# Attention with a maximum per chunk: a block's last exponential behind its stage's first tile, its factors behind the next block's first maximum

## The chip, the core and the metric

The kernel runs on one core of a Trainium2 chip. The metric is the time of one execution in microseconds (us) of device time. The core has five engines with a queue of their own each: TensorE (PE; PEld is its weight load), VectorE (DVE), ScalarE (ACT), GpSimd (POOL) and SyncE (SP), which issues nearly all DMAs. Each engine works through its queue in order; semaphores tie the queues together.

## What is computed

One decoder block over 2048 tokens of 1024 channels: a projection of the normalised input, a convolution branch, an attention branch with 8 heads, and a merge of both. The change touches the softmax of the attention branch alone:

```python
def block(args):                       # one block of 128 queries, all heads
    qn_b, qr_b, i = args
    scores = (einsum('bqhd,bkhd->bhqk', qn_b, k_nope)
              + einsum('bqhd,bkd->bhqk', qr_b, k_rope)) * scale
    scores = where(mask, scores, -inf)  # a query sees no later key
    p = softmax(scores, axis=-1)
    return einsum('bhqk,bkhd->bqhd', p, v)
```

## The kernel before

The attention stage (`attention_phase`, from L1142) works head by head: seven heads in a hardware loop, the eighth written out behind it (`last_body`). The 2048 queries are 16 blocks of 128, and four blocks form a group g; block b of group g sees g+1 chunks of up to 512 keys, and the last chunk is cut to (b+1)*128 keys. The groups come in the order 0, 3, 1, 2 (`ORDER`), so blocks s = 0 to 3 have one chunk, 4 to 7 four, 8 to 11 two, 12 to 15 three. A tile is a group's four blocks by 128 keys. The tiles of a head, T0 to T39, are 4 of g=0, 16 of g=3, 8 of g=1, 12 of g=2.

fp32 products are made of pairs in a rounded format: each operand is split in a high half (a copy on ScalarE) and a low half (a subtract on VectorE, or on GpSimd for the values and weights), and three products are added up. For one block the steps are:

- TensorE: `scores` (L1464), per chunk five products and, in the last chunk, the mask, into a bank of a ring of 5 (`ps_ring`). `ring_wait` lets a chunk start once the exponential five chunks before it is done (`exp_done`).
- VectorE, at the event `S`: the negative maximum per chunk (L1652, to `nmax`), then the least of these (L1658, to `nbias`, `max_done`). With one chunk, g=0, the first goes straight to `nbias`.
- ScalarE, at `E`: exp(score + nbias) from the bank to `prob`, with the row sum to `rsum` (L1586), for all chunks of the block. It waits for `max_done`.
- VectorE, at `E`: sum of the row sums (L1664) and reciprocal (L1670) to `rinv`.
- GpSimd, at `E`: each chunk of `prob` times `rinv` in place (L1719).

A tile at `T`: TensorE transposes it, 128x128 at a time (L1500), into one of two banks `ps_t`; ScalarE copies the high half (L1594, `pt_hi`), VectorE makes the low half (L1675, `pt_lo`). TensorE may transpose a tile once the `pt_lo` two tiles before it is done, and for the first tile that uses a chunk, once that chunk of the group's last block is normalised (`normed`). At `PV`, two tiles behind `T`, TensorE multiplies by the values (L1515 to L1517). At a group's last tile VectorE multiplies the sum by the gate (L1683), and SyncE stores it.

What sets the order is a list of events written out by `plan` (L1183) and `with_tail` (L1208). Every engine walks the same list and does its part of each event. Before, stage s of the list is S of block s, E of block s-1, and then a few tiles: 0, 1, 1, 2 in stages 4 to 7 (tiles T0 to T3), 0, 2, 7, 7 in stages 8 to 11 (T4 to T19), 0, 2, 3, 3 in stages 12 to 15 (T20 to T27). T28 to T39 come behind the list, between the next head's projections (QN, QR, K), in the last head straight behind it. The list also places `W` (splitting the next head's weights, stage 5), `VS` (splitting a quarter of the values, L1574 and L1710; stages 6 and 7 and the tail), and in the last head `OW` and `OA`: a piece of weights and the eight pieces of `o_v` that the output stage starts with (`o_a`: a copy on ScalarE, a subtract on VectorE). The `OA` pieces stand in pairs behind the events E of blocks 11 to 14. `o_v` is loaded once group 0 is stored.

## Time and profile before

| what | us |
|---|---|
| median of 3 runs (2697.78 to 2698.86) | 2698.16 |
| the profiled execution's own time | 2704.03 |
| its span, first to last instruction | 2702.2 |
| attention stage, TensorE's part of it | 1341 to 2165 |
| one head of the loop | 101.5 |
| TensorE busy | 2586.2 (96%) |
| VectorE busy | 1755.0 (65%) |
| ScalarE busy | 850.5 (31%) |
| GpSimd busy | 640.9 (24%) |

The rows below come from several views of the same execution. A row of the timeline gives the start in us from the span's start, the length in us, the engine, the line of the kernel, the operation with the buffers that it writes and reads, its shape, how many follow each other without a pause (x), and in brackets the idle time of the engine before it with what ended it. A row of the busy times gives a stretch, its length, the busy us of PE, PEld, DVE, ACT and POOL with the number of instructions, the granted TensorE clock as a share of full speed, and the share and GB/s of the DMA engines. Matmuls are pipelined: a 128x512 one shows a length of 0.39 us while the next starts 0.23 us behind it, so a short wait can hide in it.

### The profile page before, as it was taken

Reading aid. Unit: us, or ns where it says so; the run is one execution under the profiler, and the core shown is the slowest. Engines: PE = TensorE matmul, PEld = TensorE weight load, DVE = VectorE, ACT = ScalarE, POOL = GpSimd, SP = SyncE. Lnnn points to the kernel's source line nnn. Section 1 sums busy time; section 2 is a strip of 40 time slices with the busy share of each in tenths; the row PEclk is TensorE's granted clock in tenths of the full one; section 3 lists DMA queues with packets and bytes.
Section 4 is the critical chain, followed back from the end, with each engine's and each line's share of the span. In section 5 each row is a group of like instructions: output and inputs, shape, how many; then the busy total and the mean of one; then the engine's idle time right before and its main releaser. Section 6 shows DMA issues by size and latency. Waiting matters only on the chain. (4 is left out here: it accounts for less than half of the span.)

```text
span 2702.2 us, 32620 instructions
## 1 busy us (share of the span) xinstructions
PE 2586.2 (96%) x12186; PEld 2127.4 (79%) x12186; DVE 1755.0 (65%) x2073; ACT 850.5 (31%) x1683; POOL 640.9 (24%) x592
## 2 busy tenths in 40 slices
PE   4989999999999999997899999999999999999998
PEld 4767888888888888786677877877878778888887
DVE  5777967979779789564277667667677622223442
ACT  3432111111111111232255555555555520201221
POOL 3132111111111111232032232232232320323422
PEclk8999999999999999999899999999999999999999
DMA  8053212122112121376923112112112164666542
GB/s 298 8 164 116 78 47 78 47 67 83 53 55 78 47 78 48 124 243 240 278 73 107 62 60 107 62 60 107 61 61 86 55 202 156 205 215 211 190 149 78
DMA packets 200833, 306.74 MB, mean 114 GB/s; under 512 B 18234, under 2 KB 119678, under 8 KB 190621
## 3 DMA queue, kind: packets, MB, share of 16 engines
q1 hardware_dynamic: 194604, 284.89, 32.1%
q0 software_dynamic: 6128, 20.45, 2.4%
q8 instruction: 70, 1.15, 0.2%
q14 instruction: 31, 0.25, 0.0%
HBM read 202.01 MB, written 103.28 MB: 113 GB/s over the span
## 5 line engine op out<-in xcount | busy, mean ns | idle before, releaser
L52 PE MATMUL ps_proj<-h_hi,w_hi 128*128 128x512 f32 x1696 | 670.6, 395 | 9.0 <-DVE h_lo L697 6.8
L54 PE MATMUL ps_proj<-h_hi,w_lo 128*128 128x512 f32 x1696 | 663.1, 391 | 0.0
L53 PE MATMUL ps_proj<-h_lo,w_hi 128*128 128x512 f32 x1696 | 663.0, 391 | 0.0
L812 DVE SCALAR_TENSOR_TENSOR acc<-u,taps_t,acc 128x2048 f32<-128x2048 f32 x240 | 629.0, 2621 | 8.5
L52 PEld LDWEIGHTS ps_proj<-h_hi,w_hi 128*128 128x128 f32 x1696 | 320.7, 189 | 77.9 <-issue 8.0
L53 PEld LDWEIGHTS ps_proj<-h_lo,w_hi 128*128 128x128 f32 x1696 | 320.7, 189 | 67.9 <-issue 2.5
L54 PEld LDWEIGHTS ps_proj<-h_hi,w_lo 128*128 128x128 f32 x1696 | 320.2, 189 | 67.4
L586 POOL TENSOR_TENSOR w_lo<-raw,w_hi 128x1024 fp32r<-128x1024 f32 x53 | 168.4, 3177 | 808.5 <-ACT w_hi L411 808.4
L1719 POOL TENSOR_SCALAR prob<-prob,rinv 128x512 f32<-128x512 f32 (+2 forms) x320 | 199.0, 638 | 352.3 <-DVE rinv L1670 352.1
L1675 DVE TENSOR_TENSOR pt_lo<-ps_t,pt_hi 128x512 fp32r<-128x512 f32 (+1 forms) x320 | 194.1, 609 | 96.8 <-ACT pt_hi L1594 93.1
L1594 ACT ACTIVATE pt_hi<-ps_t 128x512 fp32r<-128x512 f32 (+1 forms) x320 | 169.4, 532 | 237.6 <-PE ps_t L1500 237.6
L1652 DVE TENSOR_REDUCE nmax<-ps_ring 128x1 f32<-128x512 f32 (+3 forms) x288 | 174.6, 622 | 96.1 <-PE ps_ring L1485 78.0
L539 ACT ACTIVATE lat<-ps_proj 128x512 f32<-128x512 f32 x128 | 76.3, 598 | 493.6 <-PE ps_proj L54 429.2
L2005 DVE TENSOR_TENSOR o_y<-o_ps,o_g 128x512 f32<-128x512 f32 x64 | 43.9, 690 | 265.2 <-PE o_ps L54 201.2
L1586 ACT ACTIVATE prob<-ps_ring,nbias 128x512 f32<-128x512 f32 (+2 forms) x320 | 195.3, 625 | 37.5 <-DVE nbias L1658 33.1
L52 PE MATMUL o_ps<-o_a_hi,o_w_hi 128*128 128x512 f32 x512 | 199.8, 390 | 3.4 <-DVEq L1996 3.4
L53 PE MATMUL o_ps<-o_a_lo,o_w_hi 128*128 128x512 f32 x512 | 199.9, 390 | 0.0
L54 PE MATMUL o_ps<-o_a_hi,o_w_lo 128*128 128x512 f32 x512 | 199.8, 390 | 0.0
L1500 PE MATMUL ps_t<-ident,prob 128*128 128x128 f32 x1088 | 173.3, 275 | 14.9 <-POOL prob L1719 9.5
L1500 PEld LDWEIGHTS ps_t<-ident,prob 128*128 128x128 f32 x1088 | 131.4, 141 | 48.2 <-POOL prob L1719 12.2
L1515 PE MATMUL ps_o<-pt_hi,v_hi 128*128 128x512 f32 (+1 forms) x320 | 141.4, 442 | 0.7 <-DVE bg L1683 0.7
L1480 PE MATMUL ps_ring<-kn_hi,qn_hi 128*128 128x512 f32 (+2 forms) x320 | 125.3, 392 | 8.4 <-ACT prob L1586 5.0
(220 smaller groups left out, 4037.8 us busy)
## 6 DMA issues: line engine op xcount, KB each, us to landing
qlat<-qlat_dram SPq DMA_DIRECT2D x32, 1024.0 KB, 5.9
raw<-in_w_in_dram SPq DMA_DIRECT2D x52, 512.0 KB, 6.4
under_h<-in_w_ada_dram SPq DMA_DIRECT2D x8, 1024.0 KB, 11.2
ga_dram<-lat SPq DMA_DIRECT2D x8, 1024.0 KB, 5.0
gb_dram<-lat SPq DMA_DIRECT2D x8, 1024.0 KB, 5.0
agate_dram<-lat SPq DMA_DIRECT2D x8, 1024.0 KB, 5.0
conv_dram<-acc SPq DMA_DIRECT2D x8, 1024.0 KB, 3.9
bgate_dram<-lat SPq DMA_DIRECT2D x8, 1024.0 KB, 5.0
```

The lines of the kernel that those rows point to most:

```text
L52: pe.matmul(out, wh, xh, start=first, stop=False)
L53: pe.matmul(out, wh, xl, start=False, stop=False)
L54: return pe.matmul(out, wl, xh, start=False, stop=last)
L586: pool.tensor_tensor(weights(tile)[1][:], raw[tile % 2][:], weights(tile)[0][:].bitcast(F32), ALU.subtract).then_inc(lo_made, 1)
L812: dve.scalar_tensor_tensor(acc[:], u[:, n:n + S], tap(n), acc[:], ALU.mult, ALU.add).then_inc(conv_tap if n < TAPS - 1 else conv_done, 1)
L1500: mm = pe.transpose(ps_t[:, n % 2, b * P:(b + 1) * P], prob[:, x:x + P], k.ident[:])
L1515: pe.matmul(out, v_hi[:, j, :], mh, start=(j == 0), stop=False)
L1586: act.activation(prob[:, x:x + width], ps[:, chunk_no[n, c] % RING, 0:width], ACT.Exp, bias=nbias[:, n:n + 1], accum_out=rsum[:, n, c:c + ...
L1594: act.activation(pt_hi[n % SLOTS][:, s], ps_t[:, n % 2, s], ACT.Copy).then_inc(t_hi, 1)
L1652: ins = dve.tensor_reduce(to, ps[:, chunk_no[n, c] % RING, 0:width], AX.X, ALU.max, negate=True)
L1675: dve.tensor_tensor(pt_lo[n % SLOTS][:, s], ps_t[:, n % 2, s], pt_hi[n % SLOTS][:, s].bitcast(F32), ALU.subtract).then_inc(t_lo, 1)
L1719: pool.tensor_scalar(prob[:, x:x + width], prob[:, x:x + width], rinv[:, n:n + 1], 1.0, ALU.mult, ALU.mult).then_inc(normed, 1)
```

## The change

The exponential of a chunk of g > 0 no longer uses the maximum of the block but the chunk's own (bias `nmax[:, n, c]`), and waits for that alone (`max_step`). The chunk's share, exp(chunk maximum - block maximum), is made by a small extra exponential on ScalarE over the g+1 chunk maxima (`share_of`). VectorE's `factors` multiplies the chunk sums by the shares, adds them, takes the reciprocal, and multiplies the shares by it: four dependent small steps where there were two. GpSimd then scales each chunk by its own factor. For g = 0 there is one chunk, and only the reciprocal remains.

In the list, E of block s moves from stage s+1 to stage s, in two parts: `EA`, all chunks but the last, straight behind `S`, and `E`, the last chunk and the shares, behind the stage's first tile if it has one (on ScalarE behind that tile's high half). VectorE's factors of block s-1, which stood behind all maxima of block s, now stand behind its first one. `R` is the last block's factors and scaling, behind the last stage's tiles. `W`, `VS`, `OW` and `OA` stand behind E as before, so the last head's `OA` pieces move one stage earlier with it: pairs in stages 11 (behind T13), 12, 13 (behind T20) and 14 (behind T22).

```diff
--- before.py
+++ after.py
@@ -1193,16 +1193,18 @@
 
         share = {3: [0, 1, 1, 2], 1: [0, 2, 7, 7], 2: [0, 2, 3, 3]}
         for s, (g, b) in enumerate(BLOCKS):
-            ev.append(("S", s))
-            if s:
-                ev.append(("E", s - 1))
+            ev += [("S", s), ("EA", s)]
+            n = share[g][b] if g in share else 0
+            if n:
+                tiles(1)
+                n -= 1
+            ev.append(("E", s))
             if s == 5:
                 ev.append(("W", 0))
             if s in (6, 7):
                 ev.append(("VS", s - 4))
-            if g in share:
-                tiles(share[g][b])
-        ev.append(("E", len(BLOCKS) - 1))
+            tiles(n)
+        ev.append(("R", len(BLOCKS) - 1))
         return ev, tiles, pend
 
     def with_tail(last):
@@ -1265,6 +1267,7 @@
         nmax = sb("nmax", [P, 16, NC_], F32)
         nbias = sb("nbias", [P, 16], F32)
         rsum = sb("rsum", [P, 16, NC_], F32)
+        share_of = sb("share_of", [P, 16, NC_], F32)
         rinv = sb("rinv", [P, 16], F32)
         ps = ctx.enter_context(nc.psum_tensor("ps_ring", [P, RING, TC], F32))
         ps_t = ctx.enter_context(nc.psum_tensor("ps_t", [P, 2, TC], F32))
@@ -1289,6 +1292,7 @@
         max_done = sem("max_done")
         exp_done = sem("exp_done")
         sum_step = sem("sum_step")
+        share_done = sem("share_done")
         rinv_done = sem("rinv_done")
         normed = sem("normed")
         t_done = sem("t_done")
@@ -1573,19 +1577,26 @@
                                                              + PV_CREDIT))
                             act.activation(v_hi[:, n * QB:(n + 1) * QB, :], v_raw[n % 2][:],
                                            ACT.Copy).then_inc(v_hi_made, 1)
-                        elif kind == "E":
+                        elif kind in ("EA", "E"):
                             g, b = BLOCKS[n]
-                            act.wait_ge(max_done, at.block(n + 1))
-
-                            if b == 0:
+                            n_max = chunk_no[n, 0] - QB
+                            if b == 0 and kind == "EA":
                                 held = {0: 0, 3: 0, 1: first_tile[3], 2: first_tile[1]}[g]
                                 act.wait_ge(t_done, at.tile(held + T_CREDIT))
-                            for c in range(g + 1):
+                            for c in range(g) if kind == "EA" else (g,):
                                 width = TC if c < g else (b + 1) * P
                                 x = (p_at(g, b) + c * QB) * P
+                                if g:
+                                    act.wait_ge(max_step, at.i * (N_CHUNK - QB) + n_max + c + 1)
+                                else:
+                                    act.wait_ge(max_done, at.block(n + 1))
                                 act.activation(prob[:, x:x + width], ps[:, chunk_no[n, c] % RING, 0:width], ACT.Exp,
-                                               bias=nbias[:, n:n + 1],
+                                               bias=nmax[:, n, c:c + 1] if g else nbias[:, n:n + 1],
                                                accum_out=rsum[:, n, c:c + 1]).then_inc(exp_done, 1)
+                            if g and kind == "E":
+                                act.wait_ge(max_done, at.block(n + 1))
+                                act.activation(share_of[:, n, 0:g + 1], nmax[:, n, 0:g + 1], ACT.Exp, scale=-1.0,
+                                               bias=nbias[:, n:n + 1]).then_inc(share_done, 1)
                         elif kind == "T":
                             g, j = TILES[n]
                             s = slice(max(0, j - QB * g) * P, TC)
@@ -1602,6 +1613,23 @@
             def _(dve):
                 dve.sem_inc(t_lo, LO_CREDIT)
                 dve.sem_inc(o_done, O_CREDIT)
+
+                def factors(at, n):
+                    g, b = BLOCKS[n]
+                    dve.wait_ge(exp_done, at.scores(chunk_no[n, g] + 1))
+                    if g:
+                        done = at.i * (3 * (16 - QB)) + 3 * (n - QB)
+                        sums, shares = rsum[:, n, 0:g + 1], share_of[:, n, 0:g + 1]
+                        dve.wait_ge(share_done, at.i * (16 - QB) + (n + 1 - QB))
+                        dve.tensor_tensor(sums, sums, shares, ALU.mult).then_inc(sum_step, 1)
+                        dve.wait_ge(sum_step, done + 1)
+                        dve.tensor_reduce(rinv[:, n:n + 1], sums, AX.X, ALU.add).then_inc(sum_step, 1)
+                        dve.wait_ge(sum_step, done + 2)
+                        dve.reciprocal(rinv[:, n:n + 1], rinv[:, n:n + 1]).then_inc(sum_step, 1)
+                        dve.wait_ge(sum_step, done + 3)
+                        dve.tensor_scalar(shares, shares, rinv[:, n:n + 1], None, ALU.mult).then_inc(rinv_done, 1)
+                    else:
+                        dve.reciprocal(share_of[:, n, 0:1], rsum[:, n, 0:1]).then_inc(rinv_done, 1)
 
                 def run(ev, at, prol=False):
                     number = order_of(ev)
@@ -1652,22 +1680,15 @@
                                 ins = dve.tensor_reduce(to, ps[:, chunk_no[n, c] % RING, 0:width], AX.X, ALU.max,
                                                         negate=True)
                                 ins.then_inc(max_step if g else max_done, 1)
+                                if n and c == 0:
+                                    factors(at, n - 1)
                             if g:
                                 n_max = chunk_no[n, g] + 1 - QB
                                 dve.wait_ge(max_step, at.i * (N_CHUNK - QB) + n_max)
                                 dve.tensor_reduce(nbias[:, n:n + 1], nmax[:, n, 0:g + 1], AX.X,
                                                   ALU.min).then_inc(max_done, 1)
-                        elif kind == "E":
-                            g, b = BLOCKS[n]
-                            dve.wait_ge(exp_done, at.scores(chunk_no[n, g] + 1))
-                            if g:
-                                dve.tensor_reduce(rinv[:, n:n + 1], rsum[:, n, 0:g + 1], AX.X,
-                                                  ALU.add).then_inc(sum_step, 1)
-                                dve.wait_ge(sum_step, at.i * (16 - QB) + (n + 1 - QB))
-                                src = rinv[:, n:n + 1]
-                            else:
-                                src = rsum[:, n, 0:1]
-                            dve.reciprocal(rinv[:, n:n + 1], src).then_inc(rinv_done, 1)
+                        elif kind == "R":
+                            factors(at, n)
                         elif kind == "T":
                             g, j = TILES[n]
                             s = slice(max(0, j - QB * g) * P, TC)
@@ -1709,14 +1730,15 @@
                             v = slice(n * QB, (n + 1) * QB)
                             pool.tensor_tensor(v_lo[:, v, :], v_raw[n % 2][:], v_hi[:, v, :].bitcast(F32),
                                                ALU.subtract).then_inc(v_lo_made, 1)
-                        elif kind == "E":
+                        elif kind == "R" or kind == "S" and n:
+                            n -= kind == "S"
                             g, b = BLOCKS[n]
                             pool.wait_ge(rinv_done, at.block(n + 1))
                             pool.sem_inc(passed, 1)
                             for c in range(g + 1):
                                 width = TC if c < g else (b + 1) * P
                                 x = (p_at(g, b) + c * QB) * P
-                                pool.tensor_scalar(prob[:, x:x + width], prob[:, x:x + width], rinv[:, n:n + 1], 1.0,
+                                pool.tensor_scalar(prob[:, x:x + width], prob[:, x:x + width], share_of[:, n, c:c + 1], 1.0,
                                                    ALU.mult, ALU.mult).then_inc(normed, 1)
 
                 run(prologue, At(-1), prol=True)
```

## Rows read from the trace of the kernel before

**Rows 1.** Busy time of the second head: start:end, its length, then each engine.

```profile
1462.48:1564.04 101.56, 99.24 (x546) 81.63 (x546) 72.67 (x149) 56.48 (x139) 31.36 (x45) 1.00 0.22 76
```

**Rows 2.** Waits of TensorE, attention stage: total us, times, longest us.

```profile
PE ps_t L1500 <- POOL prob L1719: 9.5, 9, 3.2
PE ps_ring L1480 <- ACT prob L1586: 5.0, 24, 0.3
```

**Rows 3.** Timeline of TensorE, block 5: start us, length us, engine, line, operation.

```profile
1472.04 0.40 PE L1485 MATMUL ps_ring<-kr_lo,qr 128*128 128x512 f32 x1
1472.70 0.50 PE L1480 MATMUL ps_ring<-kn_hi,qn_hi 128*128 128x512 f32 x1 [0.26 <-ACT prob L1586]
1473.03 0.39 PE L1481 MATMUL ps_ring<-kn_lo,qn_hi 128*128 128x512 f32 x1
1473.26 0.40 PE L1482 MATMUL ps_ring<-kn_hi,qn_lo 128*128 128x512 f32 x1
```

**Rows 4.** Timeline of TensorE: T4, the first tile of g=3.

```profile
1492.62 0.66 PE L1500 MATMUL ps_t<-ident,prob 128*128 128x128 f32 x4 [0.78 <-POOL prob L1719]
```

**Rows 5.** Timeline of GpSimd: blocks 7 and 8 are normalised.

```profile
1491.87 3.71 POOL L1719 TENSOR_SCALAR prob<-prob,rinv 128x512 f32<-128x512 f32 x6
```

**Rows 6.** Timeline of VectorE, block 10.

```profile
1495.34 0.68 DVE L1683 TENSOR_TENSOR bg<-ps_o,bg 128x512 f32<-128x512 f32 x1
1495.94 1.16 DVE L1652 TENSOR_REDUCE nmax<-ps_ring 128x1 f32<-128x512 f32 x2
...
1497.21 0.14 DVE L1664 TENSOR_REDUCE rinv<-rsum 128x1 f32<-128x2 f32 x1
1497.39 0.16 DVE L1670 RECIPROCAL rinv<-rinv 128x1 f32<-128x1 f32 x1
1497.62 0.69 DVE L1675 TENSOR_TENSOR pt_lo<-ps_t,pt_hi 128x512 fp32r<-128x512 f32 x1
```

**Rows 7.** Timeline of ScalarE in the output stage: a small activation and its follower.

```profile
2566.76 0.29 ACT L1960 ACTIVATE o_ss<-o_ss,eps 128x1 f32<-128x1 f32 x1
2566.96 1.66 ACT L1935 ACTIVATE o_a_hi<-o_v 128x512 fp32r<-128x512 f32 x3
```

**Rows 8.** Timeline of ScalarE, last head, blocks 13 and 14.

```profile
2130.07 0.60 ACT L1594 ACTIVATE pt_hi<-ps_t 128x512 fp32r<-128x512 f32 x1 [0.20 <-PE ps_t L1500]
2130.57 0.68 ACT L1586 ACTIVATE prob<-ps_ring,nbias 128x512 f32<-128x512 f32 x1
...
2131.23 0.69 ACT L1586 ACTIVATE prob<-ps_ring,nbias 128x512 f32<-128x512 f32 x1
...
2131.89 0.48 ACT L1586 ACTIVATE prob<-ps_ring,nbias 128x256 f32<-128x256 f32 x1
...
2132.34 1.17 ACT L1562 ACTIVATE o_a_hi<-o_v 128x512 fp32r<-128x512 f32 x2
```

**Rows 9.** Timeline of TensorE: end of two chunks, and T8 and T24.

```profile
1490.77 0.39 PE L1485 MATMUL ps_ring<-kr_lo,qr 128*128 128x512 f32 x1
...
1498.62 0.49 PE L1500 MATMUL ps_t<-ident,prob 128*128 128x128 f32 x3
...
1518.79 0.39 PE L1485 MATMUL ps_ring<-kr_lo,qr 128*128 128x512 f32 x1
...
1526.77 0.60 PE L1500 MATMUL ps_t<-ident,prob 128*128 128x128 f32 x4
```

**Rows 10.** Timelines of GpSimd and VectorE at one time.

```profile
1464.02 1.29 POOL L1710 TENSOR_TENSOR v_lo<-v_raw,v_hi 128x512 fp32r<-128x512 f32 x1 [7.82 <-ACT v_hi L1574]
...
1464.11 1.74 DVE L1640 TENSOR_TENSOR qr<-rope_a,qr 64x512 fp32r<-64x512 f32 x1
```

**Rows 11.** Timeline of TensorE, last head: T27.

```profile
2144.41 0.33 PE L1500 MATMUL ps_t<-ident,prob 128*128 128x128 f32 x1 [0.95 <-DVE pt_lo L1675]
```

**Rows 12.** TensorE in the last head: T28, and the stretch behind it.

```profile
2148.45 0.66 PE L1500 MATMUL ps_t<-ident,prob 128*128 128x128 f32 x4 [3.19 <-POOL prob L1719]
...
2149.20:2156.00 6.80, 6.14 (x24) 5.05 (x23) 2.92 (x5) 2.39 (x4) 0.53 (x1) 0.50 0.16 54
```

## The prediction

> **What bounds the kernel now.** I read the busy time by head first. The second head takes 101.56 us and TensorE is busy for 99.24 of it at full clock; VectorE is busy for 72.67 and ScalarE for 56.48 [rows 1]. So the attention stage is bound by TensorE's matmuls, and the change alters no matmul. All it can do is remove or add waits of TensorE. Next I read what TensorE waits for in this stage, over all eight heads. It waits for a normalised piece of `prob` 9 times, 9.5 us in all, one of them 3.2 us, and for an exponential that frees a bank of the score ring 24 times, 5.0 us [rows 2]. Then I read TensorE in order of time around each wait, since part of a wait hides in the modelled length of a matmul; the distance between starts is the better measure. Below, blocks are s = 0 to 15 and tiles T0 to T39 of a head in the order of the lists; all times are of the second head unless said.
>
> *Ring waits.* Neighbouring 512-column matmuls start 0.23 us apart (1473.03 to 1473.26). Before the second chunk of block 5 the distance is 0.66 us, and 0.33 behind it, so this wait costs 0.43 + 0.10 = 0.53 us [rows 3]. The like places in blocks 6 and 7 cost 0.47 and 0.44 by the same distances. Block 4's (0.39) hangs on the head's first exponential. That is not moved, so it stays.
>
> *The wait for GpSimd.* T4, the first tile of g=3, starts at 1492.62 after 0.78 us of shown idle [rows 4]; by the distance of starts it is 0.95, and 0.05 in the next transposes: 1.00 us. GpSimd ran from 1491.87 on block 7's chunks [rows 5], and in before's order a v_lo piece stood in front of them on its queue.
>
> **What the change takes away, per head.** Chunks 0 to 2 of a four-chunk block now go through the exponential as soon as their own maximum is known, within the block's own stage. The bank that the next block's second chunk wants is free more than 1 us early. Gone: 0.53 + 0.47 + 0.44 = 1.44 us. Block 7's factors are computed behind the first maximum of block 8. That maximum ends at about 1490.1, v_lo holds GpSimd to about 1490.3, the four small steps end at 1490.9, and the first chunk is normalised at 1491.6. T4 wants it at 1491.68 (0.94 before 1492.62): the wait falls to 0.05. Gone: 0.95. Sum of the gains: **2.4 us per head**.
>
> **What it adds, per head: small steps on two queues.**
> VectorE: per block of g>0 a multiply over 2 to 4 columns and a multiply by a pointer scalar, beside the sum and reciprocal that were there. No row shows such small multiplies; the nearest are the sum and the reciprocal. Dependent steps follow at 0.18 us (1497.21 to 1497.39), the work behind the last at about 0.08 [rows 6]. Old: 0.26. New: 3 x 0.19 + 0.08 = 0.65. The extra is 0.39 us; bounds 0.2 (a step at half) and 1.2 (each new step held up by GpSimd once, below). All four now stand between the first and second maximum.
> ScalarE: per block an exponential of 2 to 4 values. Nearest row: a 128x1 activation with a bias takes 0.29 and the next begins 0.20 behind its start [rows 7]. I take 0.20; bounds 0.08 (a 512-column copy's 0.49 less 512 columns' worth) and 0.29.
> 12 blocks have these, 4.7 and 2.4 us per head of engines with 29 and 45 us idle. As sums they cost nothing. As links of a chain they may cost: a tile's copy (ScalarE) and remainder (VectorE) stand on the same queues, and the tile two places on cannot be transposed before.
>
> *The wait at T8.* Other lengths: 512 exponential to next 0.67, 256 columns 0.45, copy 0.60 (to next 0.49) [rows 8]; maximum or remainder 0.69 (to next 0.61), gate multiply to next 0.60 [rows 6]. A finished engine releases the next in 0.04, and TensorE in 0.15. Block 9's first chunk leaves TensorE at 1491.16 [rows 9]. Maximum to 1491.90. Factors of block 8: 1491.82 to 1492.47, or to 1492.93 with GpSimd's hold-up. Maximum of 256 columns to 1493.41. Last exponential from 1493.45, share from 1493.90, copy of T5 1494.10 to 1494.70, remainder 1494.73 to 1495.42, gate multiply from 1495.34, block 10's first maximum 1495.94 to 1496.63. Its exponential from 1496.67, copy of T6 1497.33 to 1497.93, remainder 1497.96 to 1498.65. T8 can start at 1498.80. Without T4's wait TensorE would want T8 at 1498.62 - 0.94 = 1497.68. So it waits **1.12**, and 0.11 follows: 1.23 us. Without GpSimd's hold-up 0.75. In the old order this copy stood ahead of the block's exponentials, so the cover was there.
>
> *The hold-up.* VectorE's 64x512 subtract with two inputs in SBUF usually takes 0.69, but 1.74 where GpSimd's 1.29 us operation had started 0.09 before it, and it ended 0.54 behind that one [rows 10]. Factor steps that fall into GpSimd's run of block 7's four chunks should wait likewise: 0.46 in the walk. The Trainium skill ("SBUF — State Buffer", Who interferes with whom) says that a VectorE instruction with two SBUF inputs, or a tensor_scalar in its two-port mode, and a GpSimd instruction that reads SBUF exclude each other for the whole instruction. By that rule both new multiplies would be held and T8 waits 1.12; the trace agrees for two inputs and shows nothing for the pointer multiply.
>
> *The wait at T24.* Block 13's second chunk leaves TensorE at 1519.18. The factors of block 12 hold VectorE to 1519.33. Maximum to 1520.02; exponential from 1520.06; copy of T20 1520.73 to 1521.33; last exponential (256) 1521.22; share 1521.67; copy of T21 1521.87 to 1522.47; remainder to 1523.19; gate multiply from 1523.11; block 14's first maximum 1523.71 to 1524.40; factors to 1524.97; second maximum to 1525.66; exponential from 1525.70; copy of T22 1526.37 to 1526.97; remainder to 1527.69; T24 at 1527.84. Now it starts at 1526.77 [rows 9], so it waits **1.07**, with 0.06 behind. T16 comes out 0.08 late; T27 is in time.
>
> **Sum.** Per head -2.39 + 1.23 + 1.13 + 0.08 = +0.05: the waits change place. Seven heads: +0.3.
> *Last head.* It has two waits of its own, at T24 and T27 (0.95 shown at T27 [rows 11], 1.05 and 1.17 by starts). They come from the o_a pieces, two copies in 1.17 us on ScalarE [rows 8] and as many subtracts on VectorE behind each pair, and they move. Gone with the rest: 2.4 + 1.05 + 1.17. T28's wait (3.19 shown, 3.36 by starts [rows 12]) falls to about 1.8, as block 15's exponentials are done before its last tiles. Sum 6.2. Added: the 1.23 at T8; T16 1.3, since two o_a pieces now stand in front of T14's copy; T23 1.0; T24 3.5, as four pieces delay blocks 13 and 14 by 2 us each way. Sum 7.0 to 7.4. Net +1.0. Behind the 3.19 us of idle the granted clock was 0.50 for 6.8 us [rows 12]; I expect one such stretch again, behind T24 in place of T28: no difference. If it falls out, 3.2 us are gained; if there are two, 3 lost.
> Against the profiled run (2704.03): 2704.03 + 0.3 + 1.0 = 2705.3. That run is 5.9 above the median of 2698.16, so I forecast **2699.5**.
>
> **The rivals.**
> *B, the new waits are small.* Both walks end on ScalarE and VectorE steps 0.04 to 0.2 long that I can't see. If shares cost 0.08, the factor steps 0.1 each, and GpSimd holds nothing, T8's and T24's waits come to half: 8 x 1.2 = 9.6, so 2698.2 - 9.6 = 2689 (2685 to 2692). For it: VectorE is idle for 29 us a head, and much of that lies in front of the second maxima, where TensorE needs 1.14 us a chunk and VectorE 0.61. Against: the walks have no idle step.
> *C, slower: factors in front of the second maximum.* Where GpSimd is still normalising, each of the two multiplies may wait a whole chunk (0.62), and the second maximum, its exponential and the next tile's copy move with it. Its place is blocks 8 to 10, and 13 to 14 through the gate multiply. It decides once the factors of block 8 take more than 1.1 us, or those of 13 more than 0.65. At 0.6 us more in each head at either place: 8 x 1.2 = 9.6, so 2708 (2704 to 2712).
> *D, the ring waits stay,* because an exponential now waits for its own chunk's maximum, while the new waits come: 8 x 1.4 = 11, so 2710. Against: by the walk the bank is free over 1 us early.
>
> **Chances.** Forecast (2693 to 2704) 0.47, B 0.28, C 0.20, D 0.05. Range 8 in 10: 2687 to 2709. A measurement here can tell 0.2% (5.4 us) from no change: faster below 2692.8, slower above 2703.6. Faster 0.28, same 0.47, slower 0.25.
>
> **What would show it.** Right: no wait for an exponential at the second chunks of blocks 5 to 7, T4's wait below 0.2, and in every head new waits for pt_lo of 0.8 to 1.3 us at T8 and T24; heads of 101.3 to 102.0 us. B: such waits below 0.6 and heads near 100.3. C: above 1.5 and heads over 102.5. The four factor steps should lie 0.19 apart where GpSimd is idle, and be stretched in block 8's. The forecast fails if a wait that I did not walk opens elsewhere (T16, T27, the first projections of the next head), or if the o_v load has not landed when ScalarE reaches the first o_a piece, one stage earlier than now.

## The result: 2706.65 us, slower by 0.27%

The changed kernel takes 2706.65 us (median of 8 runs, 2705.14 to 2708.09) where the kernel before takes 2699.05 in the same comparison. The ratio is 1.0027, with an interval of 1.0017 to 1.0037: 4.6 to 10 us slower. The forecast was 2699.5, so the time is inside the range and on the slower side of the forecast, where I had put a chance of 0.25.

The profiled execution took 2707.97 us, against 2704.03 before. That difference (3.9) is smaller than the one in the medians (7.6). The stage that the change touches gives a cleaner one: from the first score to the end of the last head's last product it takes 804.3 us before (1360.96 to 2165.29) and 810.5 after (1358.81 to 2169.29), so **6.2 us more**. Ahead of attention, where nothing was changed, the changed kernel's profiled run is 2.2 us shorter, and that is why the profiled executions differ by less.

The page of the changed kernel, its span and the busy time of its engines:

```profile
span 2706.2 us, 33319 instructions
PE 2577.3 (95%) x12186; PEld 2122.9 (78%) x12186; DVE 1800.8 (67%) x2265; ACT 873.8 (32%) x1779; POOL 639.9 (24%) x592
```

The second and the last head of the changed kernel, by windows (stretch, its length, busy time and instructions of PE, PEld, DVE, ACT and POOL, granted clock, DMA share, GB/s):

```profile
1461.55:1563.88 102.33, 98.58 (x547) 81.68 (x546) 78.42 (x173) 59.45 (x151) 31.51 (x45) 1.00 0.22 76
2075.65:2169.29 93.64, 83.78 (x474) 68.24 (x473) 67.23 (x159) 56.05 (x146) 30.74 (x44) 1.00 0.19 63
```

The second head has grown from 101.56 [rows 1] to 102.33 us; a head is counted from its first score to that of the next. TensorE has no more work, but VectorE has 78.42 where it had 72.67. The other heads follow: the first one 102.74 (101.52 before), the five behind the second 102.33 to 102.37. The last one is 93.64 (93.50 before). By heads: 1.2 + 6 x 0.8 + 0.14 = 6.1 of the 6.2 us.

What the tiles and their products wait for in the attention stage, all heads (total us, times, longest):

```profile
PE ps_t L1504 <- POOL prob L1741: 17.0, 17, 1.9
PE ps_t L1504 <- DVE pt_lo L1696: 13.8, 17, 1.9
PE ps_o L1519 <- DVE bg L1704: 3.1, 3, 2.2
```

Before, the exponentials' ring waits stood here with 24 entries and `prob` with 9.5 us [rows 2]. The ring waits are gone. The wait for GpSimd's `prob`, which was to vanish, has grown to 17.0, in 17 places instead of 9.

### The profile page after: what moved, and what is told of

Its sections match the earlier page's. It is cut to its first block and busy times, and to the rows that moved or that the text cites. A ratio compares the mean times of both kernels' runs of the same rounds, so it can differ in the third digit from the quotient of the medians.

```text
span 2706.2 us, 33319 instructions
## 1 busy us (share of the span) xinstructions
PE 2577.3 (95%) x12186; PEld 2122.9 (78%) x12186; DVE 1800.8 (67%) x2265; ACT 873.8 (32%) x1779; POOL 639.9 (24%) x592
## 5 line engine op out<-in xcount | busy, mean ns | idle before, releaser
L1741 POOL TENSOR_SCALAR prob<-prob,share_of 128x512 f32<-128x512 f32 (+2 forms) x320 | 196.2, 628 | 323.5 <-DVE share_of L1630 305.2
L1593 ACT ACTIVATE prob<-ps_ring,nmax 128x512 f32<-128x512 f32 (+3 forms) x288 | 182.2, 634 | 151.8 <-DVE nmax L1680 150.9
```

The source lines that it names most:

```text
L1593: act.activation(prob[:, x:x + width], ps[:, chunk_no[n, c] % RING, 0:width], ACT.Exp, bias=nmax[:, n, c:c + 1] if g else nbias[:, n:n + 1 ...
L1741: pool.tensor_scalar(prob[:, x:x + width], prob[:, x:x + width], share_of[:, n, c:c + 1], 1.0, ALU.mult, ALU.mult).then_inc(normed, 1)
```

## The second head, wait by wait

TensorE in order of time (start, length, then the idle time before it and its releaser in brackets): the second chunk of block 5, then T4, T8 and T24.

```profile
1470.71 0.39 PE L1489 MATMUL ps_ring<-kr_lo,qr 128*128 128x512 f32 x1
1470.94 0.40 PE L1484 MATMUL ps_ring<-kn_hi,qn_hi 128*128 128x512 f32 x1
...
1490.58 0.66 PE L1504 MATMUL ps_t<-ident,prob 128*128 128x128 f32 x4 [1.59 <-POOL prob L1741]
...
1497.15 0.52 PE L1504 MATMUL ps_t<-ident,prob 128*128 128x128 f32 x3 [0.42 <-POOL prob L1741]
...
1526.59 0.63 PE L1504 MATMUL ps_t<-ident,prob 128*128 128x128 f32 x4 [0.96 <-DVE pt_lo L1696]
```

The starts at block 5's second chunk are 0.23 apart where they were 0.66 [rows 3]. T4 shows 1.59 where it showed 0.78 [rows 4], and T8 and T24 [rows 9] now wait. By distance of starts, in us:

| place | before | forecast | after |
|---|---|---|---|
| ring waits, blocks 4 to 7 | 1.85 | 0.39 | 0 |
| T4 | 1.00 | 0.05 | 1.81 |
| T8 | 0 | 1.23 | 0.58 |
| T16 | 0 | 0.08 | 0.05 |
| T24 | 0 | 1.13 | 1.13 |

The differences add up: -1.85 + 0.81 + 0.58 + 0.05 + 1.13 = +0.72 of the head's +0.77.

*T8's releaser* is named GpSimd, but VectorE's remainder of T6 ends at 1497.00, 0.15 before T8's start:

```profile
1496.31 0.69 DVE L1696 TENSOR_TENSOR pt_lo<-ps_t,pt_hi 128x512 fp32r<-128x512 f32 x1
```

That is the gap at which TensorE follows VectorE here; GpSimd's `prob` had long been there. This is the chain that the forecast walked.

*T4's releaser* is GpSimd in earnest. GpSimd in order of time, with its idle time before each step:

```profile
1476.87 1.84 POOL L1723 TENSOR_TENSOR head_w_l<-head_raw,head_w_h 128x768 fp32r<-128x768 f32 x1 [1.74 <-ACT head_w_h L1550]
1478.95 2.48 POOL L1741 TENSOR_SCALAR prob<-prob,share_of 128x512 f32<-128x512 f32 x4 [0.24 <-DVE share_of L1630]
1482.54 1.29 POOL L1731 TENSOR_TENSOR v_lo<-v_raw,v_hi 128x512 fp32r<-128x512 f32 x1 [1.12 <-ACT v_hi L1578]
...
1487.66 1.29 POOL L1731 TENSOR_TENSOR v_lo<-v_raw,v_hi 128x512 fp32r<-128x512 f32 x1 [1.01 <-ACT v_hi L1578]
1489.83 3.71 POOL L1741 TENSOR_SCALAR prob<-prob,share_of 128x512 f32<-128x512 f32 x6 [0.88 <-DVE share_of L1630]
```

VectorE's factor steps over the same time:

```profile
1472.32 0.23 DVE L1630 TENSOR_SCALAR share_of<-share_of,rinv 128x4 f32<-128x4 f32 x1
...
1477.23 1.51 DVE L1630 TENSOR_SCALAR share_of<-share_of,rinv 128x4 f32<-128x4 f32 x1
1478.65 1.74 DVE L1680 TENSOR_REDUCE nmax<-ps_ring 128x1 f32<-128x512 f32 x3
...
1482.87 0.99 DVE L1630 TENSOR_SCALAR share_of<-share_of,rinv 128x4 f32<-128x4 f32 x1
...
1487.99 0.68 DVE L1680 TENSOR_REDUCE nmax<-ps_ring 128x1 f32<-128x512 f32 x1
1488.59 0.38 DVE L1624 TENSOR_TENSOR rsum<-rsum,share_of 128x4 f32<-128x4 f32 x1
```

The pointer multiply over 4 columns takes 0.23 when GpSimd is free. Block 4's does. Block 5's takes 1.51: GpSimd's `head_w_l` subtract began 0.36 before it and ended at 1478.71, and the multiply ended at 1478.74. Block 6's takes 0.99 and ends 0.03 behind the v_lo subtract (1483.83, 1483.86). Behind each stand the second, third and fourth maximum of the next block, and behind these its exponentials. ScalarE shows it:

```profile
1463.02 1.28 ACT L1593 ACT_TABLE_LOAD   x1
1465.27 0.37 ACT L1593 ACTIVATE prob<-ps_ring,nbias 128x128 f32<-128x128 f32 x1 [0.96 <-DVE nbias L1680]
...
1479.37 0.69 ACT L1593 ACTIVATE prob<-ps_ring,nmax 128x512 f32<-128x512 f32 x1 [1.82 <-DVE nmax L1680]
```

It sits 1.82 us for a maximum. All that follows is late: the copies for `VS`, thus GpSimd's v_lo at 1487.66, the remainder at 1487.78, block 8's first maximum at 1487.99. The late v_lo then lies over the first factor step (0.38 instead of 0.15). The factors are done at 1489.6, GpSimd starts at 1489.83, and T4 at 1490.58.

The first two rows bear on block 4's ring wait, which I had left standing. The table load of the exponentials now begins at 1463.02 and is over when the first maximum comes. In the kernel before it ran behind the wait for that maximum:

```profile
1466.28 1.28 ACT L1586 ACT_TABLE_LOAD   x1 [2.33 <-DVE nbias L1652]
1467.57 0.37 ACT L1586 ACTIVATE prob<-ps_ring,nbias 128x128 f32<-128x128 f32 x1
```

The likely reason is that the diff swaps two waits in front of this exponential. `max_done` came first, then `t_done`; now `t_done` stands in `EA` and `max_done` in `E`. The load would stand behind the first wait and ahead of the second in both. No run tried this alone, so the reason is not shown. With the load out of the way block 4's 0.39 us is gained, which no step of the forecast holds.

## The experiments

Two accounts stood against each other. **P:** the last factor step, a multiply by a pointer scalar, is held by GpSimd's long subtracts, and this is T4's wait. **Its rivals:** the new order on ScalarE, in which a block's exponentials stand between a tile's two copies, or the mere length of the small steps. Each expectation says what either account would give. Head lengths below are those of the second head (before 101.56, after 102.33), and waits of tiles are by distance of starts. The diffs show the main lines of each edit, with other lines left out. Run 4 edits the kernel before and run 8 the kernel of run 5, the others edit the changed kernel. Runs 1 to 9 were executed once each.

The changed kernel holds one such comparison itself. Its last head has no next head's weights to split, so `head_w_l` is not there. Block 5's multiply is not held in it, only block 6's (0.98 us), and T4 waits 0.51 instead of 1.81.

**1. No pointer multiply on VectorE.** GpSimd's instruction takes both factors, so the step falls out.

```diff
-                        dve.tensor_scalar(shares, shares, rinv[:, n:n + 1], None, ALU.mult).then_inc(rinv_done, 1)
-                                pool.tensor_scalar(prob[:, x:x + width], prob[:, x:x + width], share_of[:, n, c:c + 1], 1.0,
+                                pool.tensor_scalar(prob[:, x:x + width], prob[:, x:x + width], rinv[:, n:n + 1],
+                                                   share_of[:, n, c:c + 1] if g else 1.0,
```

> The changed kernel without VectorE's last factor step: GpSimd's scaling takes the reciprocal and the chunk's share as its two scalars. In the changed kernel that step took 1.51 us in block 5 and 0.99 in block 6 (0.23 elsewhere), ending 0.03 behind a GpSimd operation. Theory P (VectorE's last step is shut out by GpSimd's long subtracts, the second maxima and all behind them slip, and with them block 7's normalising): those 1.3 and 0.8 us vanish, T4's wait falls from 1.76 us to at most 0.4, T8's rises from 0.58 towards 1.1 as TensorE is no longer late, T24's stays at 1.0 to 1.13; heads of 101.2 to 101.6 us instead of 102.36. Rival Q (the places in the queues do it: v_lo stands behind the later exponentials, and the port has no part): T4's wait stays above 1.3 us and heads at 102.2 or more.

It took 2694.46 us in one run, beside 2702.51 for the kernel before. Its second head:

```profile
1459.51:1560.02 100.51, 98.54 (x547) 81.71 (x546) 75.31 (x161) 60.13 (x151) 34.45 (x45) 1.00 0.22 77
```

T4's wait is down from 1.81 to 0.12, T24's fell from 1.13 to 0.74, and T8's is 0.78. The rival by which the places in the queues do it, with T4 above 1.3, is out: those places are the same here. The step that is removed is worth 1.8 us a head. GpSimd pays with 34.45 busy us instead of 31.51. The gain is larger than expected: the four-step chain became three, so T24 profits as well.

**2. Factors behind the last maximum,** not the first.

```diff
-                                if n and c == 0:
-                                    factors(at, n - 1)
+                            if n:
+                                factors(at, n - 1)
```

> The changed kernel with VectorE's factors of the block before behind all maxima of a block, as in the kernel before; all else as changed. Theory P: a held step no longer stops the maxima, so T4's wait falls from 1.76 to 0.3 to 0.7 us (block 7's factors come 0.3 later than they could). Of the chain that ends at T24 the 0.65 us of factors before the second maximum of block 14 and 0.11 in block 13 fall out: T24's wait 1.13 goes to about 0.4. T8's about 0.5. Heads near 100.9 us. Rival Q: T4's wait stays above 1.3 us; T24's falls all the same.

It took 2705.2 us, and its second head 102.03 instead of the expected 100.9. One row of its VectorE, then two of its GpSimd:

```profile
1484.87 1.39 DVE L1630 TENSOR_SCALAR share_of<-share_of,rinv 128x4 f32<-128x4 f32 x1
```
```profile
1484.41 0.59 POOL L1741 TENSOR_SCALAR prob<-prob,share_of 128x384 f32<-128x384 f32 x1
1484.96 1.28 POOL L1731 TENSOR_TENSOR v_lo<-v_raw,v_hi 128x512 fp32r<-128x512 f32 x1
```

T24's wait fell to 0.32, as expected: the steps no longer stand in front of the second maximum. In its place T15 waits 0.28 and T27 0.47. T4's did not fall to the expected 0.3 to 0.7; it is 1.75, which is the rival's condition. Block 7's own multiply is held here, and ends 0.02 behind v_lo. But that is not what makes T4 late: v_lo stands in front of block 7's chunks on GpSimd's own queue until 1486.24, and GpSimd starts on them at 1486.47, so the held multiply costs T4 about 0.2. The late factors of block 6 had pushed v_lo there: GpSimd sat 1.25 us idle for them, and v_lo followed their chunks without a pause. So the place that helps T24 makes GpSimd's queue late. What this run says of T4 is neither for P nor against it.

**3. No shares at all** (and two factor steps as before). This kernel leaves out the weighting of the chunks: each is scaled by the reciprocal of the plain sum, which is not the softmax. It gives the price of the small steps.

```diff
-                                act.activation(share_of[:, n, 0:g + 1], nmax[:, n, 0:g + 1], ACT.Exp, scale=-1.0,
-                                               bias=nbias[:, n:n + 1]).then_inc(share_done, 1)
-                        dve.tensor_tensor(sums, sums, shares, ALU.mult).then_inc(sum_step, 1)
-                        dve.tensor_scalar(shares, shares, rinv[:, n:n + 1], None, ALU.mult).then_inc(rinv_done, 1)
```

> Leaves out the shares: each chunk is scaled by the reciprocal of the plain sum, so the chunks of a row are weighted wrongly; 12 small exponentials per head on ScalarE and 24 small multiplies on VectorE are gone, the order is that of the changed kernel. It gives the price of the small steps. Theory (both steps as links of the chain to T24: 0.20 of share, 0.39 and 0.11 of factors): T24's wait falls from 1.13 to about 0.4; T4's to at most 0.3, as nothing of VectorE is shut out. Heads near 100.7 us. Rival: the order alone makes the waits (a tile's copy behind the exponentials of its own block): T24 stays above 0.9.

It took 2684.09 us, with a second head of 99.69: the small steps together cost 2.6 us a head. T4 waits 0 and T24 0.36, where 0.4 was expected. T8 still waits 0.60, where run 5, with T4's wait all but gone too, has 0.80. So two thirds of T24's wait are made by the small steps, and three quarters of T8's are not: they are left to the new order of exponentials and copies.

**4. The kernel before, with its v_lo splits earlier,** in stages 4 and 6 instead of 6 and 7. It has none of the new small steps, so it shows how much of the wait at T4 before came from GpSimd's queue.

```diff
-            if s in (6, 7):
-                ev.append(("VS", s - 4))
+            if s in (4, 6):
+                ev.append(("VS", 2 + (s == 6)))
```

> The kernel before with the values' splits moved from stages 6 and 7 to 4 and 6, so that no v_lo stands in front of block 7's scaling on GpSimd. If T4's wait of 0.95 us there comes from that alone, it goes to 0.0 to 0.1 us, heads of 100.6 us instead of 101.55, 7 to 8 us in all; if it comes from block 7's late exponentials, it stays above 0.7.

It took 2697.26 us. Its second head took 101.06 where 100.6 was expected. Its GpSimd, then its TensorE, at T4:

```profile
1488.26 2.04 POOL L1719 TENSOR_SCALAR prob<-prob,rinv 128x512 f32<-128x512 f32 x3 [0.62 <-DVE rinv L1670]
```
```profile
1489.01 0.55 PE L1500 MATMUL ps_t<-ident,prob 128*128 128x128 f32 x3 [0.20 <-POOL prob L1719]
```

GpSimd no longer has v_lo in front of the chunks: it sits 0.62 us idle for the reciprocal, and VectorE had in turn waited for the block's last exponential. T4's wait fell from 1.00 to 0.42 and not to nothing. So of the wait of before, GpSimd's queue made about 0.6, and the block's late exponentials the rest.

**5. The changed kernel with its splits early.** The same change that P asks for: `W` and `VS` directly behind `S`, ahead of the exponentials, so that GpSimd's subtracts are over when the factors come.

```diff
             ev.append(("S", s))
+            if s == 5:
+                ev.append(("W", 0))
+            if s in (6, 7):
+                ev.append(("VS", s - 4))
```

> The changed kernel with W and the two VS events directly behind S instead of behind E, so that ScalarE copies the weights and values ahead of the block's exponentials and GpSimd's long subtracts end before VectorE's factor steps. All factor steps stay. Theory P (a factor step that meets a GpSimd operation waits for its end): the last step takes 0.23 us in blocks 4 to 7, no second maximum slips, T4's wait falls from 1.76 to 0.0 to 0.3 us, T8's rises to 0.8 to 1.1, T24's stays 1.1; heads of 100.8 to 101.4 us. Rival Q (the added step and its place alone, with no shut-out): heads as in the changed kernel, 102.3.

It took 2697.33 us (before 2698.06). The pointer multiply over all heads (count, then shortest, median and longest in ns), first in the changed kernel, then with the splits early:

```profile
L1630 DVE TENSOR_SCALAR share_of<-share_of,rinv x96: 228/229/1516, 1369.9 to 2153.4; 128x4 f32<-128x4 f32 x32, 128x2 f32<-128x2 f32 x32, 128x3 f32<-128x3 f32 x32
```
```profile
L1631 DVE TENSOR_SCALAR share_of<-share_of,rinv x96: 228/229/277, 1368.4 to 2143.4; 128x4 f32<-128x4 f32 x32, 128x2 f32<-128x2 f32 x32, 128x3 f32<-128x3 f32 x32
```

The longest falls from 1516 to 277 ns, T4's wait from 1.81 to 0.16, and the head from 102.33 to 101.16. T24 stays at 1.13. T8 rises to 0.80, since TensorE now comes to it earlier, and 0.20 appears at a product behind T4. P holds: all small steps are there and in their places, and with the overlap gone nearly all of T4's wait is gone. This edit changes ScalarE's order too and alone would leave the rival standing; run 1 keeps that order.

**6. Odd columns.** The multiply over 4 columns is cut in 3 and 1, to see whether the hold-up depends on an even width.

```diff
-                        dve.tensor_scalar(shares, shares, rinv[:, n:n + 1], None, ALU.mult).then_inc(rinv_done, 1)
+                        for part in (slice(0, 3), slice(3, 4)) if g == 3 else (slice(0, g + 1),):
+                            ins = dve.tensor_scalar(share_of[:, n, part], share_of[:, n, part], rinv[:, n:n + 1], None,
+                                                    ALU.mult)
```

> The changed kernel with the last factor step of a four-chunk block in two parts, three columns and one. It asks which form of that step GpSimd can shut out. If only an even number of elements can use VectorE's second port (a two-port mode), the parts are not held: 0.16 to 0.23 us each in blocks 5 and 6, T4's wait falls to 0.4 or less, heads near 101.4 us. If any pointer multiply is held, the first part takes the 1.5 and 1.0 us as before and heads stay at 102.3 to 102.5.

It took 2711.88 us with a head of 102.74, slower than the changed kernel. The same view as above:

```profile
L1631 DVE TENSOR_SCALAR share_of<-share_of,rinv x128: 199/228/1510, 1367.4 to 2156.5; 128x3 f32<-128x3 f32 x64, 128x1 f32<-128x1 f32 x32, 128x2 f32<-128x2 f32 x32
```

The longest is still 1510 ns, and it is a part of three columns (8 of them at 0.97 to 0.99, 7 at 1.50 to 1.51). An odd width does not escape, and the added instruction makes T4's wait longer, 2.18.

**7. The o_a pieces later.** In the last head they go behind the next stage's `S`, as late as before.

```diff
-                ev.insert(ev.index(("E", 11 + t // 2)) + 1 + t % 2, ("OA", t))
+                ev.insert(ev.index(("S", 12 + t // 2)) + 1 + t % 2, ("OA", t))
```

> The changed kernel with the last head's o_a pieces one stage later (behind S of blocks 12 to 15), where they stood before the change in time. Theory: the waits of the last head at T16 (1.34), at the first product of T20 (2.41) and at T24 (2.09) come from these pieces. T16's goes to below 0.1; the other two together from 4.5 to 2.5 or less, with about 1 us new at T27: the last head is 2.5 to 4 us shorter than 93.6 us; the others are unchanged at 102.3.

It took 2704.3 us. Its last head:

```profile
2074.00:2165.60 91.60, 83.54 (x474) 68.20 (x473) 68.03 (x159) 56.36 (x146) 33.15 (x44) 1.00 0.20 64
```

The last head is 2.0 us shorter than after's 93.64, less than the 2.5 to 4 expected. The wait at T16 is down to 0.11 and the one of the product is gone, but T24 now waits 2.78 and T27 1.10. The pieces have to be copied and subtracted somewhere; they moved the wait more than they removed it.

**8. One tile ahead of the exponentials,** on top of 5. If T8's wait came from the exponentials standing ahead of the first tile's copy, this would end it.

```diff
+            if n:
+                tiles(1)
+                n -= 1
             ev.append(("EA", s))
-            if n:
-                tiles(1)
-                n -= 1
             ev.append(("E", s))
```

> The kernel of run splits_early with a stage's first tile ahead of the block's exponentials (S, tile, EA, E, other tiles). It tests the order on ScalarE's queue, with all small steps kept. Theory (T8 and T24 wait because the copy of T6 and T22 stands behind exponentials of its own block): T24's wait falls from 1.13 to below 0.2 and T8's from 0.80 to below 0.2; the second tile's copy now stands behind all of them, so T9 and T15 or T16 wait 0.4 to 0.8 each; small ring waits (0 to 0.3) can return at blocks 6 and 7. Heads of 100.2 to 101.0 us instead of 101.16. Rival (the small steps make the waits, wherever the copy stands): T24 stays above 0.7.

This expectation failed. It took 2728.33 us, with a second head of 104.30. T24 waits 1.25 and T8 0.72, neither below the expected 0.2; T16 waits 0.72, T4 1.33, and ring waits are back at blocks 6 and 7. The largest waits of that head, then one row of its ScalarE and one of its VectorE:

```profile
PE ps_t L1505 <- DVE pt_lo L1697: 2.1, 3, 1.1
PE ps_t L1505 <- POOL prob L1742: 1.7, 2, 1.1
PE ps_ring L1485 <- ACT prob L1594: 0.4, 2, 0.2
```
```profile
1493.32 0.29 ACT L1606 ACTIVATE pt_hi<-ps_t 128x128 fp32r<-128x128 f32 x1
```
```profile
1493.64 0.29 DVE L1697 TENSOR_TENSOR pt_lo<-ps_t,pt_hi 128x128 fp32r<-128x128 f32 x1 [2.32 <-ACT pt_hi L1606]
```

The first tile's copy is early, but the second one's now stands behind all of the block's exponentials and the share. VectorE waits 2.32 us for it, and with VectorE all the maxima behind. So moving the exponentials to the other side of the first copy does not end the wait. The recorded rival, by which the small steps make the waits wherever the copy stands, has its condition met (T24 above 0.7), but by run 3 T8 keeps 0.60 without those steps. That the waits come from exponentials standing between two copies of one stage at all fits the rows; no run tests it alone.

**9. The mixture.** Blocks 0 to 7 as changed (early exponentials, chunk maxima), with both factors on GpSimd and the splits early. Few tiles compete for ScalarE there. Blocks 8 to 15 in the order of before, with one maximum and one factor.

```diff
+            if s < EARLY:
+                ev.append(("EA", s))
+                ...
+                ev.append(("E", s))
+            elif s > EARLY:
+                ev += [("EA", s - 1), ("E", s - 1)]
```

> A mixture: blocks 0 to 7 as in the changed kernel (maximum by chunk, own stage), but with GpSimd applying both factors and the splits directly behind S; blocks 8 to 15 in the order of the kernel before (block maximum, exponentials one stage later, sum and reciprocal behind the maxima). Theory: the ring waits (1.85 us) and T4's wait (0.95) are gone and no wait at T8 and T24 comes, since there the tile's copy stands ahead of its own block's exponentials again: heads of 98.6 to 99.2 us, the whole about 20 us below the kernel before. Rival: T8's and T24's waits come from the state in which blocks 5 to 7 leave the queues, and stay at 0.5 or more: heads above 99.8.

It took 2678.29 us in one run. Its second head, and what TensorE waits for in it:

```profile
1455.81:1554.50 98.69, 97.94 (x546) 81.87 (x546) 74.11 (x153) 57.91 (x143) 32.89 (x45) 1.00 0.22 78
```
```profile
PE ps_t L1509 <- DVE pt_lo L1701: 0.5, 1, 0.5
PE ps_ring L1489 <- DVE kn_lo L1653: 0.3, 1, 0.3
```

The ring waits, T4's, T8's and T24's are all gone. What is left is T32's, which before has too. The head is 2.87 us shorter than before's, and the waits of before that are gone are 1.85 + 1.00 = 2.85. Its edit changes the order, the small steps and the splits together, so it does not say which of them frees T8 and T24. But it shows that the gains that I forecast were there to be had; the held multiply and the new waits at T8 and T24 gave them back.

**10 to 12. Timed.** The mixture again, the kernel of run 1, and the mixture with the last head's o_a pieces each behind one of the last eleven tiles (`OA` t behind tile T(29+t)).

> The mixture of run early_group3 again, timed: its heads were 98.68 us against 101.55, so 8 x 2.87 = 23 us at most and 19.8 in that single look. Theory: 0.9915 to 0.9935 of the kernel before.

> The changed kernel with the chunk's two factors applied by GpSimd, timed: heads of 100.5 us against 101.55. Theory: the change's only loss was the last factor step shut out by GpSimd, so without that step it is faster than the kernel before, 0.996 to 0.998. Rival: the last head takes back what the seven give, 0.999 or more.

> The mixture with the last head's o_a pieces behind tiles T29 to T36 instead of in stages 12 to 15. Theory: the waits at T24 (1.06) and T27 (1.12) of the last head vanish, VectorE's two 0.6 us steps per tile against TensorE's 1.13 cost 0.1 a tile in the tail, so 1 to 2 us less than the mixture. Rival: the tail becomes bound by VectorE and the output stage starts no earlier: no difference.

| kernel | median us | ratio to before (2699.42) |
|---|---|---|
| both factors on GpSimd | 2691.75 | 0.9969, 0.9957 to 0.9981 |
| mixture | 2678.41 | 0.9927, 0.9914 to 0.9941 |
| mixture, o_a at the tail | 2675.65 | 0.9911, 0.9898 to 0.9925 |

All three are faster than both kernels of this case. The last two can't be told apart by their intervals, but their last heads can. First the mixture's, then that with the pieces at the tail:

```profile
2045.90:2138.10 92.20, 86.19 (x474) 71.48 (x473) 62.37 (x140) 55.12 (x138) 34.81 (x44) 0.94 0.20 64
```
```profile
2048.85:2138.50 89.65, 84.91 (x474) 70.22 (x473) 62.52 (x139) 54.92 (x138) 31.93 (x44) 0.96 0.21 65
```

The difference of 2.55 us is about that of the medians (2.8), where 1 to 2 were expected. The waits at T24 and T27 are gone, which are the forecast's 1.05 and 1.17; besides, a product behind them waits 0.6 longer, and the stretch at half clock is shorter. Such a stretch is left in each: the granted clock is 0.50 from 2120 to 2125 in the first, and 0.61 in the mean from 2120 to 2128 in the second. The attention stage of the last kernel takes 780.9 us against 804.3, 23.4 less; the medians differ by 23.8.

## Where the forecast held and where it failed, by its own steps

The time lies in the range, but the reason given for it failed at T4, and that the whole still fits is partly luck, as the last head shows.

**Right: the ring waits.** They went, by more than counted: 1.85 a head, not 1.44. The step "Block 4's (0.39) hangs on the head's first exponential. That is not moved, so it stays" failed. The exponential wasn't moved, but the load of its table was.

**Wrong: T4.** "T4 wants it at 1491.68: the wait falls to 0.05" is the step that failed, and the one that decided. It came to 1.81 in each of the seven heads of the loop, an error of 1.76 us, and to 0.51 in the last. The walk took GpSimd's v_lo as something in front of the chunks on GpSimd's queue, and did not look at what GpSimd's subtracts do to VectorE. The text had the mechanism and its upper bound ("each new step held up by GpSimd once"), but placed it at block 8 alone, where GpSimd scales. The factors of blocks 5 and 6 and the subtracts `head_w_l` and v_lo, which the change had moved behind `E` with everything else, I never laid side by side. The shown price is 0.76 to 1.28 us for a step of 0.23, where I had 0.46. Run 1 takes away the step and run 5 the overlap, and T4's wait is down to 0.12 and 0.16. In run 2 the step is held at another place, where v_lo on GpSimd's own queue was the larger hindrance.

The Trainium skill ("SBUF — State Buffer", Who interferes with whom) says that a VectorE tensor_scalar in its two-port mode and a GpSimd instruction exclude each other for the whole instruction. The trace agrees: 0.99 and 1.51 instead of 0.23, ended 0.03 behind GpSimd. The forecast drew on this rule and applied it to one place of three. By the same page the one that issues first has the ports. In run 2 the multiply's row begins 0.09 before v_lo's and is yet held for 1.39; but GpSimd's chunk of 1484.41 was still running until 1484.99, and v_lo followed it without a pause. So that row is no case of VectorE coming first. The Trainium skill ("VectorE: DVE Perf Modes", What auto-detection actually checks) lets odd widths into this mode if source and destination are equal. Run 6 agrees, with three columns at 1.51.

**Half right: T8.** Forecast 1.23, or 0.75 without GpSimd's hold-up; measured 0.58 behind T4's wait, and 0.80 where that is gone (run 5). The hold-up of 0.46 in block 8's factors did not come in the seven heads of the loop, though GpSimd was scaling just then. It came in the last head. The multiply with two inputs and the GpSimd chunk beside it, first in the second head, then in the last:

```profile
1490.49 0.70 POOL L1741 TENSOR_SCALAR prob<-prob,share_of 128x512 f32<-128x512 f32 x1
1490.56 0.15 DVE L1624 TENSOR_TENSOR rsum<-rsum,share_of 128x2 f32<-128x2 f32 x1
...
2103.29 0.70 POOL L1741 TENSOR_SCALAR prob<-prob,share_of 128x512 f32<-128x512 f32 x1
2103.39 0.60 DVE L1624 TENSOR_TENSOR rsum<-rsum,share_of 128x2 f32<-128x2 f32 x1
```

Begun 0.06 behind GpSimd's row it takes its usual 0.15, begun 0.10 behind it takes 0.60 and ends with GpSimd's. The pointer multiply falls on the seam between two chunks and takes 0.24. So the loop's heads missed this hold-up by a few hundredths of a us, which no walk of the kernel before could foresee. What remains is the walk's second value. Run 3 shows that only about 0.2 of it comes from the small steps.

**Right: T24 and T16.** 1.13 against 1.13, and 0.05 against 0.08. The chain that was walked is the one in the trace. VectorE in block 14, between its first and second maximum:

```profile
1523.02 0.15 DVE L1624 TENSOR_TENSOR rsum<-rsum,share_of 128x3 f32<-128x3 f32 x1
...
1523.59 0.23 DVE L1630 TENSOR_SCALAR share_of<-share_of,rinv 128x3 f32<-128x3 f32 x1
1523.73 1.15 DVE L1680 TENSOR_REDUCE nmax<-ps_ring 128x1 f32<-128x512 f32 x2
```

The four steps take 0.71 from the first to the maximum behind them (0.65 assumed), and the share's exponential delays the next copy by 0.19 (0.20 assumed). Runs 2 and 3 cut this wait to 0.32 and 0.36, by moving the steps out of the chain and by removing them.

**The last head.** Net +0.14, forecast +1.0. TensorE in it, at T16, at a product that waits for the gate multiply, at T24 and T28:

```profile
2123.90 0.63 PE L1504 MATMUL ps_t<-ident,prob 128*128 128x128 f32 x4 [1.18 <-DVE pt_lo L1696]
...
2141.14 0.50 PE L1519 MATMUL ps_o<-pt_hi,v_hi 128*128 128x512 f32 x1 [2.16 <-DVE bg L1704]
...
2145.15 0.63 PE L1504 MATMUL ps_t<-ident,prob 128*128 128x128 f32 x4 [1.92 <-DVE pt_lo L1696]
...
2154.62 0.66 PE L1504 MATMUL ps_t<-ident,prob 128*128 128x128 f32 x4 [1.95 <-POOL prob L1741]
```

By starts T16 waits 1.34 (forecast 1.3). The first product of T20 and T24 wait 2.41 and 2.09, 4.5 together; the forecast had the same sum, cut in 1.0 at T23 and 3.5 at T24. T28 waits 2.12, down from 3.36, against "about 1.8". These sizes were good. T4's 0.51 instead of 0.05, and 0.43 and 0.20 at a product behind T4 and at T12, were in no step. The expected stretch at half clock fell out: the granted clock of this head rounds to 1.00, where before had 0.50 for 6.8 us [rows 12]. The longest idle of TensorE here is 2.16 us; before's was 3.19. That length does not settle it: in run 5's last head the same product waits 2.19, and the granted clock is 0.50 from 2131.2 to 2134.4. The forecast had valued this case at 3.2 us. Had the stretch come, this head would be near 97 by that price, 3.3 above before's and not the forecast's 1.0. So the small +0.14 is luck. The whole kernel would then have taken some 2710 us (2706.65 + 3.2, an estimate), just outside the range.

**Rivals.** C's time (2704 to 2712) came true, and its kind of mechanism: factors, held by GpSimd, in front of the second maximum. Its place did not, nor its signs: no wait at T8 or T24 of the seven heads is above 1.5, and the heads of 102.33 lie between the forecast's 102.0 and C's 102.5. It was to happen at blocks 8 to 10 and 13 to 14, while GpSimd scales; it happened at blocks 5 and 6, while GpSimd makes its splits. C was to decide once block 8's factors took over 1.1 us or block 13's over 0.65. Block 8's took 0.72, and block 13's the 0.71 above, over the mark but with no step held; the 1.51 was at block 5's. B and D did not come. By terms, for the seven heads: T4 +1.76, ring waits -0.41, T8 -0.65, together +0.70 a head or 4.9 us, and the last head -0.9. That is 4.0 of the 4.9 us between the forecast's +1.3 and the trace's +6.2; the first head, which grew by 1.2 where the others grew by 0.8, is another 0.4, and 0.5 stays open.

**Open.** Why the table load moved, and what exactly makes T8's 0.60, are argued and not tested. What would end T32's 0.65 us was not tried, nor why the mixture's last head still has a stretch at half clock.

## What to carry to other kernels

In this kernel a small VectorE step was priced not by its columns but by what GpSimd did at that moment: a 0.23 us multiply took up to 1.51, and it stood in front of maxima on which everything else hung. Before adding such steps to a chain, lay every GpSimd operation of that stretch beside them, those that the same edit moves included; or let GpSimd's own instruction carry the second factor.

A new order can be kept where it helps alone. Here it paid in the blocks with few tiles and cost in those with many, and using each where it pays was worth 21 us, where the whole change lost 7.6.

## What the runs showed of the hardware that I had not expected

The multiply by a pointer scalar over 4 or 3 columns was blocked for all of GpSimd's remaining subtract (0.99 or 1.51 instead of 0.23), and ended 0.02 to 0.03 behind it. A multiply with two inputs in SBUF over 4 columns went from 0.15 to 0.38 under v_lo, and one over 2 columns to 0.60 under a scaling chunk.

A few hundredths of a us decide whether a step is held: begun 0.06 behind the row of a GpSimd chunk it ran in 0.15, begun 0.10 behind in 0.60. In run 2 a multiply that began while a chunk was running was held through the subtract that followed that chunk without a pause (1.39).

A second pointer factor in GpSimd's scaling costs little: the median chunk takes 767 ns with two factors and 691 with one, both in the mixture.

The 1.28 us load of an activation table went from behind a wait of ScalarE to ahead of it in the changed kernel, in which the two waits in front of that exponential stand in the other order, and block 4's 0.39 us went with it. That the order of the waits did it was not tested alone.
